# Block B's second feed-forward layer in seven quarter products instead of eight, with partial sums copied out by ScalarE and added by GpSimd

## The reference

```python
h2 = rmsnorm(x, p['norm_ffn_g'])
u = jnp.square(jax.nn.relu(jnp.einsum('btd,df->btf', h2, p['w_up'])))
x = x + jnp.einsum('btf,fd->btd', u, p['w_down'])
```

## Time and profile before

| | |
|---|---|
| median of 3 runs | 1424.47 us (1423.86 to 1426.74) |
| profiled execution, first to last instruction | 1424.1 us, clock 0.993 |
| TensorE busy | 1375.1 us (97%) |
| VectorE, ScalarE, GpSimd busy | 834.5, 542.6, 318.1 us |
| block B's 8 groups | about 1042 to 1415 us of the span |
| one group in the middle | 46.0 us |

### The profile page before, as it was taken

One profiled execution on the slowest core, in us unless ns is written; L12 is line 12 of the kernel. 1 busy time (PEld: TensorE's weight loads), 2 busy tenths in 40 slices (PEclk: granted clock), 3 DMA queues, 4 the chain that ended last, 5 costly groups with the idle time before them and its releaser, 6 DMA issues.

```text
span 1424.1 us, 23612 instructions
## 1 busy us (share of the span) xinstructions
PE 1375.1 (97%) x8781; PEld 1145.8 (80%) x8781; DVE 834.5 (59%) x1416; ACT 542.6 (38%) x1011; POOL 318.1 (22%) x363
## 2 busy tenths in 40 slices
PE   7998999999999999998999999999999999999998
PEld 6767777776777767776767767667999999999998
DVE  5469667745648886758667564444454455445542
ACT  6444332414546554533325241332442234223431
POOL 2546624435523534342000000000220000000000
PEclk9999999999999999999999999999999999999999
DMA  8547745434255553453377565971532233123311
GB/s 273 147 129 236 219 131 169 140 120 140 89 159 168 184 174 112 132 165 121 104 240 240 190 218 174 315 245 62 179 125 76 90 119 104 60 75 119 119 31 60
DMA packets 115635, 211.99 MB, mean 149 GB/s; under 512 B 12665, under 2 KB 45722, under 8 KB 115522
## 3 DMA queue, kind: packets, MB, share of 16 engines
q1 hardware_dynamic: 104306, 176.94, 38.3%
q10 hardware_dynamic: 11216, 33.57, 7.4%
HBM read 184.00 MB, written 26.46 MB: 148 GB/s over the span
## 4 chain that ended last, share of the span: by engine, by line
PE 64%; DVE 5%; ACT 3%; issue 2%; DMA 0%; ACTq 0%; POOL 0%; SPq 0%; DVEq 0%; POOLq 0%
PE ps L85 18%; PE ps L87 17%; PE ps L86 17%; PE ps L2634 2%; PE ps L1495 2%; PE ps L1532 2%; PE ps L1314 1%; DVE uw_l L2084 1%; PE ps L1516 1%; ACT uw_h L2080 1%; DVE ul L2243 1%; PE ps L1728 1%; DVE sd L2388 1%; DVE dl L2190 1%; DVE xr L2236 0%
## 5 line engine op out<-in xcount | busy, mean ns | idle before, releaser
L85 PE MATMUL ps<-uh,dh 128*128 128x512 f32 (+2 forms) x768 | 250.0, 326 | 5.0 <-DVE dl L2190 3.9
L87 PE MATMUL ps<-uh,dl 128*128 128x512 f32 (+2 forms) x768 | 245.4, 320 | 0.0
L86 PE MATMUL ps<-ul,dh 128*128 128x512 f32 (+2 forms) x768 | 245.0, 319 | 0.0
L2399 POOL TENSOR_TENSOR kr<-kr,qb 128x512 f32<-128x512 f32 x128 | 175.9, 1385 | 167.4 <-DMA kr<-in_cache_k 167.0
L2254 DVE TENSOR_TENSOR xt<-xt,ps 128x256 f32<-128x256 f32 (+2 forms) x192 | 97.6, 512 | 164.6 <-PE ps L87 164.1
L85 PEld LDWEIGHTS ps<-uh,dh 128*128 128x128 f32 x768 | 144.4, 188 | 25.3 <-DVE xt L2254 7.6
L87 PEld LDWEIGHTS ps<-uh,dl 128*128 128x128 f32 x768 | 144.5, 188 | 11.5
L86 PEld LDWEIGHTS ps<-ul,dh 128*128 128x128 f32 x768 | 144.6, 188 | 9.7
L2095 ACT ACTIVATE dh<-raw_dn 128x1024 fp32r<-128x1024 f32 x64 | 67.5, 1055 | 215.6 <-PE ps L87 214.9
L2080 ACT ACTIVATE uw_h<-raw_up 128x1024 fp32r<-128x1024 f32 x80 | 84.5, 1056 | 163.4 <-PE ps L87 163.3
L85 PE MATMUL ps<-x2hB,uw_h 128*128 128x264 f32 (+1 forms) x512 | 145.2, 284 | 0.7 <-DVE x2lB L2218 0.7
(11 more groups left out here) (339 smaller groups left out, 2840.0 us busy)
## 6 DMA issues: line engine op xcount, KB each, us to landing
kr<-in_cache_k SPq DMA_DIRECT2D x128, 256.0 KB, 3.1
raw_up<-in_w_up_units SPq DMA_DIRECT2D x64, 512.0 KB, 4.7
vr<-in_cache_v SPq DMA_DIRECT2D x128, 256.0 KB, 3.5
raw_dn<-in_w_down ACTq DMA_DIRECT2D x62, 512.0 KB, 3.6
raw<-in_w_in_units SPq DMA_DIRECT2D x23, 512.0 KB, 5.1
raw_up<-in_w_out_units SPq DMA_DIRECT2D x16, 512.0 KB, 4.4
xin<-in_x_prompt SPq DMA_DIRECT2D x8, 512.0 KB, 5.4
xt_scratch<-xts SPq DMA_DIRECT2D x8, 512.0 KB, 5.9
```

The lines of the kernel that those rows point to most:

```text
L85: pe.matmul(out, lh, rh, start=first and n == 0, stop=False)
L86: pe.matmul(out, lh, rl, start=False, stop=False)
L87: ins = pe.matmul(out, ll, rh, start=False, stop=last and n == len(ks) - 1)
L2399: pool.tensor_tensor(k[:, :], k[:, :], qb[v // PAGES][:, :], ALU.mult).then_inc(k_multiplied, 1)
```

## The change

`feed_forward` becomes two functions: `feed_first` for block A, with the same work in the same order, and `feed_last` for block B. The `out` tiles and `up` tiles of B are the same matmuls. `down` is replaced: the 512 x 1024 piece of `w_down` of a group is taken as a 2 x 2 matrix of quarters A11, A12, A21, A22 (256 hidden features x 512 outputs, A12 and A22 belonging to the second half of the hidden features, A21 and A22 to the second half of the outputs), the squared activations as 2 x 2 quarters U11 to U22 (256 features x 256 or 264 tokens), and their product is made from seven quarter products (Winograd's form) instead of eight. Each quarter product is 4 output tiles x 2 k-steps x 3 matmuls = 24 matmuls, so `down` has 168 instead of 192. P2 and P4 have 256 columns, the other five 264.

What this needs per group, by engine:

- GpSimd: four sums or differences of weight quarters (S1 = A21+A22, S3 = A11-A21, S2 = S1-A11, S4 = A12-S2; 128x1024 elements each), and 16 additions of partial results onto `xt` (128x256 or 128x264).
- ScalarE: 7 high parts of factors instead of 4 (128x1024), 8 squares as before, 14 high parts of activations instead of 8, and 16 new copies of a PSUM bank into SBUF (`read` into `held`).
- VectorE: 7 low parts of factors instead of 4, 8 relus as before, 8 differences of activations (T1 to T4, `change`, in place), 14 low parts instead of 8, and 12 additions from PSUM onto `xt` instead of 16.
- TensorE: P1 is left in its bank, P6, P7 and P4 are accumulated onto it, P3 onto P5. In between ScalarE reads the bank, and the next product of that bank waits for that read (`y_copied`). P6 of an output tile waits for the read of P1, P7 for that of P6, P4 for that of P7, P3 for that of P5.
- SyncE: the `w_down` tiles come on its queue, all four buffers at once; ScalarE no longer issues them.
- At the end one token tile is turned inside the last group and four behind it, each with its own PSUM banks and its own SBUF place; ScalarE copies three, VectorE two.

In groups 0 to 6 TensorE's order is P1 for all four output tiles, then P5, P6, P2, P7, P3, P4 for tiles 0 and 1, then the same for tiles 2 and 3. Cut to its core:

```diff
+PRODUCTS = {"P1": ("A11", "U11", "X"), "P2": ("A12", "U21", "Y"), "P3": ("S4", "U22", "Z"), "P4": ("A22", "T4", "X"),
+            "P5": ("S1", "T1", "Z"), "P6": ("S2", "T2", "X"), "P7": ("S3", "T3", "X")}
+BEGINS = ("P1", "P5", "P2")
+AFTER = {"P6": "P1", "P7": "P6", "P4": "P7", "P3": "P5"}
+READ_OUT = ("P1", "P6", "P7", "P5")
+ADDED = ("P2", "P3", "P4")
+def products(g):
+    if g == FGROUPS - 1:
+        return [(x, j) for x in ("P1", "P6", "P2", "P7", "P5", "P4", "P3") for j in range(PAIRS)]
+    return ([("P1", j) for j in range(PAIRS)]
+            + [(x, j) for js in ((0, 1), (2, 3)) for x in ("P5", "P6", "P2", "P7", "P3", "P4") for j in js])
...
+        def product(g, x, j):
+            name, part, kind = PRODUCTS[x]
+            if x in BEGINS:
+                take(pe, "down", (g, x, j))
+            else:
+                pe.wait_ge(y_copied, read_no(g, AFTER[x], j))
+            if j == 0:
+                pe.wait_ge(dn_low, factor_no(g, name))
+            f, n = slice(j * P, (j + 1) * P), width(x)
+            for k in range(2):
+                if j == 0:
+                    pe.wait_ge(u_low, low_no(g, part, k))
+                ins = split_matmuls(pe, ps[:, down_bank(g, kind, j), 0:n],
+                                    lambda k: (factor(fh, name)[:, k, f], factor(fl, name)[:, k, f]),
+                                    lambda k: (part_place(part, k, False)[:, 0:n], part_place(part, k, True)[:, 0:n]),
+                                    [k], x in BEGINS and k == 0, k == 1, x not in BEGINS)
+            ins.then_inc(down_ready, 1)
...
+        def read(g, x, j):
+            act.wait_ge(down_ready, product_no(g, x, j))
+            if held_before(g, x, j):
+                act.wait_ge(sq_added, held_before(g, x, j))
+            if (g, x, j) == (0, "P1", 0):
+                for i in range(2):
+                    act.wait_ge(sem(f"y_out{i}"), 32)
+            if (g, x, j) == (FGROUPS - 1, "P1", 2):
+                act.wait_ge(dn_low, factor_no(g, "S2"))
+                act.wait_ge(sq_added, sum_no(g, "S4"))
+            dst = held_at(g, x, j)
+            act.activation(dst, ps[:, down_bank(g, PRODUCTS[x][2], j), 0:256 if x == "P1" else WIDE], ACT.Copy).then_inc(y_copied, 1)
...
+            todo = reads(g)
+            high_factor(g, "A11")
+            high_factor(g, "A12")
+            if g == 0:
+                split_high(act, t + 2)
+                act.wait_ge(norm_product, 4)
+                for p in range(2):
+                    ins = act.activation(rb2[:, tokens(p)], ps[:, 7 - p, 0:HALVES[p][1]], ACT.Copy)
+                ins.then_inc(rb2_made, 1)
+            square(g, 0, 0)
+            high_part(g, "U11", 0)
+            square(g, 0, 1)
+            if g:
+                split_high(act, t + 2)
+            high_part(g, "T1", 0)
+            high_factor(g, "S1")
+            high_factor(g, "S3")
+            square(g, 1, 0)
+            high_part(g, "U11", 1)
+            square(g, 1, 1)
+            split_high(act, t + 3)
+            high_part(g, "T1", 1)
+            high_factor(g, "S2")
+            high_factor(g, "A22")
+            square(g, 2, 0)
+            high_part(g, "U21", 0)
+            square(g, 2, 1)
+            if more:
+                split_high(act, t + 4)
+            for name in ("U22", "T2", "T3", "T4"):
+                high_part(g, name, 0)
+            high_factor(g, "S4")
+            square(g, 3, 0)
+            high_part(g, "U21", 1)
+            square(g, 3, 1)
+            high_part(g, "T2", 1)
+            read(g, *todo[0])
+            read(g, *todo[1])
+            high_part(g, "T3", 1)
+            high_part(g, "U22", 1)
+            read(g, *todo[2])
+            read(g, *todo[3])
+            high_part(g, "T4", 1)
+            read(g, *todo[4])
+            read(g, *todo[5])
+            if more:
+                split_high(act, t + 5)
+            for what in todo[6:]:
+                read(g, *what)
...
+        def summed(g):
+            a11, a12, a21, a22 = (quarter(x) for x in ("A11", "A12", "A21", "A22"))
+            for x in range(FT):
+                pool.wait_ge(dn_in[x], raw_no(g, x))
+            if g == 0:
+                pool.wait_ge(sem("mix_turned"), 18)
+                pool.wait_ge(sem("ods_done"), 1)
+            else:
+                pool.wait_ge(dn_low, factor_no(g - 1, "S1"))
+            pool.tensor_tensor(s1[:, :, :], a21, a22, ALU.add).then_inc(sq_added, 1)
+            pool.tensor_tensor(a21, a11, a21, ALU.subtract).then_inc(sq_added, 1)
+            pool.wait_ge(dn_low, factor_no(g, "A11"))
+            pool.wait_ge(sq_added, sum_no(g, "S3"))
+            pool.tensor_tensor(a11, s1[:, :, :], a11, ALU.subtract).then_inc(sq_added, 1)
+            pool.wait_ge(dn_low, factor_no(g, "A12"))
+            pool.wait_ge(sq_added, sum_no(g, "S2"))
+            pool.tensor_tensor(a12, a12, a11, ALU.subtract).then_inc(sq_added, 1)
+        def add(g, x, j):
+            pool.wait_ge(y_copied, read_no(g, x, j))
+            if g and x in ("P1", "P6"):
+                pool.wait_ge(added, added_no(g - 1, "P2" if x == "P1" else "P3", j))
+            if x in ("P5", "P7") and both_before(g, x, j):
+                pool.wait_ge(sq_added, both_before(g, x, j))
+            o, c = out_tile(x, j)
+            pool.tensor_tensor(xt[:, o, c], xt[:, o, c], held_at(g, x, j), ALU.add).then_inc(sq_added, 1)
...
+            low_factor(g, "A11")
+            low_factor(g, "A12")
+            relu(g, 0, 0)
+            relu(g, 0, 1)
+            low_part(g, "U11", 0)
+            change(g, "T1", 0)
+            if g:
+                split_low(dve, t + 2)
+            low_part(g, "T1", 0)
+            low_factor(g, "S1")
+            low_factor(g, "S3")
+            relu(g, 1, 0)
+            relu(g, 1, 1)
+            low_part(g, "U11", 1)
+            change(g, "T1", 1)
+            split_low(dve, t + 3)
+            low_part(g, "T1", 1)
+            low_factor(g, "S2")
+            relu(g, 2, 0)
+            relu(g, 2, 1)
+            low_part(g, "U21", 0)
+            change(g, "T2", 0)
+            change(g, "T3", 0)
+            if more:
+                split_low(dve, t + 4)
+            low_part(g, "U22", 0)
+            change(g, "T4", 0)
+            low_part(g, "T2", 0)
+            low_part(g, "T3", 0)
+            low_part(g, "T4", 0)
+            low_factor(g, "A22")
+            relu(g, 3, 0)
+            relu(g, 3, 1)
+            low_part(g, "U21", 1)
+            change(g, "T2", 1)
+            change(g, "T3", 1)
+            low_part(g, "T2", 1)
+            change(g, "T4", 1)
+            low_part(g, "T3", 1)
+            low_part(g, "U22", 1)
+            low_part(g, "T4", 1)
+            low_factor(g, "S4")
+            todo = adds(g)
+            add(g, *todo[0])
+            add(g, *todo[1])
+            if more:
+                split_low(dve, t + 5)
+            for what in todo[2:]:
+                add(g, *what)
+        for t in (1, 3):
+            copy_y(t)
```

More of the change, by code:

```diff
@@ new lines, in up @@
+            take(pe, "up", g, x)
+            for i in range(2):
+                for k in range(i * KT // 2, (i + 1) * KT // 2):
+                    if g == 0 and x == 0:
+                        pe.wait_ge(x2_low, k + 1)
+                    ins = split_matmuls(pe, ps[:, bank("up", g, x), :], weights(t),
+                                        lambda k: (x2h[:, k, ALL], x2l[:, k, ALL]), [k], k == 0, k == KT - 1)
+                    if g == 0 and x == 1 and k == 4:
+                        spread()
+                if i:
+                    ins.then_inc(up_ready, 1)
+                beside(tick + i)
@@ new lines, in down @@
+            for o in range(2):
+                take(pe, "down", g, o)
+                sum_over(o, range(3), True, False)
+            for o in range(2):
+                pe.wait_ge(u_low, up_no(g, 3) + 1)
+                sum_over(o, range(3, 4), False, True).then_inc(down_ready, 1)
+            for i in range(2):
+                beside(tick + i)
+            for o in range(2, KT):
+                take(pe, "down", g, o)
+                sum_over(o, range(FT), True, True).then_inc(down_ready, 1)
+                beside(tick + o)
@@ L2054, in tensor @@
+        first_outs()
+        for u in range(2, KT):
             out(u)
@@ L2063, in tensor @@
             tick += KT
-        if part:
-            for t in range(2, 5):
-                turn_y(t)
     def before_tile(u, beside):
@@ L2223, in vector @@
                 t = KT + FT * g + x
-                more = t + 2 < TILES or part == 0
                 beside(tick + 2 * x)
@@ L2256, in feed_forward @@
     return {"sync": sync, "tensor": tensor, "scalar": scalar, "gpsimd": gpsimd, "vector": vector,
             "split_high": split_high, "split_low": split_low, "preload": preload}
+PAIRS = KT // 2
+HALVES = [(0, 256), (256, 264)]
+WIDE = 264
+FACTORS = ["A11", "A12", "S1", "S3", "S2", "A22", "S4"]
```

(3 more changed lines are left out.)

771 lines of the change are left out of this document (529 added, 242 removed).

## The result

The kernel after takes 1435.68 us (median of 4 runs, 1432.7 to 1437.7), the kernel before on the same chip 1425.56 (1423.86 to 1426.74): a ratio of 1.0065, 95% interval 1.0044 to 1.0085. The forecast was 1435. The profiled execution of after has a span of 1435.9 us.

A forecast was written before the change was run, and what follows sets the result against it. TensorE was taken to bound block B, its saving eaten by stalls: 1424.1 + 10 (group 0) + 3 (groups 1 to 6) - 0.4 (last group) - 2.4 (end) = 1434.3, plus 0.4 from span to median: 1435 us. Range 1405 to 1458, 8 in 10.

The forecast's parts named there:

- The matmuls: TensorE's down in block B: fewer matmuls save 2.8 us a group, 22 us for the eight.
- rival 3: Accumulating onto a bank read in between costs TensorE its pitch, 168 matmuls last as long as 192: 1457 us, chance 0.05.
- The middle group: Groups 1 to 6 of block B: stalls of 3.3 us against 2.8 saved, 46.5 us a group, +3 in all.
- All four stalls: TensorE's waits in a middle group: up tile 2 0.5 us, tile 3 0.7, P6 0.8, P7 1.3.
- Turns: GpSimd and VectorE alternate at the shared SBUF port; a 1024-element sum on GpSimd holds it 2.35 us.
- rival 1: GpSimd doesn't get between VectorE's queued operations, so the port harms little: 1408 us, chance 0.34.
- The price of a sum: GpSimd's durations: 2.5 us for a sum of 1024 elements, about 0.75 for an addition of 264.
- rival 2: VectorE becomes the bound through dearer sums, pieces and hand-overs: 2.3 us more a group, 1455 us, chance 0.18.
- Group 0: Block B's first group, whose up results wait for the norm: stalls sum to 13.3 us, net +10.
- The spread: TensorE's step behind group 0's norm: waits 4.2 us because GpSimd's S1 and S3 delay VectorE's diagonal operations.
- The last group and the end: Last group -0.4 us; behind the last product fewer turns of token tiles remain, -2.4 us.
- The 0.4 us between span and median: Added to the forecast span of 1434.3 us to reach the forecast median of 1435.

The follow-up runs named there:

- The kernel without collisions: Changed kernel with GpSimd's four weight sums made over 16 columns instead of 1024, all waits kept, results wrong: 1409.71 us, ratio 0.9894.
- narrow sums: Changed kernel with GpSimd's four weight sums over 16 columns instead of 1024, all waits kept, results wrong: 1409.71 us, ratio 0.9894.
- filled sums: Changed kernel with each GpSimd weight sum replaced by three constant fills of about its length that read no SBUF, results wrong: 1410.47 us, ratio 0.989.
- narrow sums and narrow adds: Changed kernel with GpSimd's four sums over 16 columns of 1024 and its 16 additions over 8 columns, results wrong: 1406.22 us, ratio 0.9868.

## Why the prediction was right

**The matmuls (rival 3).** 2.8 us a group forecast, 2.7 measured. Accumulating onto a bank that was read in between costs nothing that these runs show, so rival (3) falls.

**The middle group.** 46.5 forecast, 46.36 measured. All four stalls were where the working had put them, behind the operations it had named. With the 0.27 us that a wait costs beyond its bracket, tile 3 lost 0.7 us (0.7 forecast), P6 0.7 (0.8) and P7 1.4 (1.3). Tile 2 lost 0.3 (0.5): 0.18 before its first matmul, which starts 0.30 behind the last one where the pitch is 0.12, and 0.1 behind it. Together 3.1 us, where 46.36 - 43.32 is 3.0 and 3.3 was forecast.

**Turns (rival 1).** The two low parts at 1150.24 decide it: GpSimd does get between two queued operations of VectorE. The kernel without collisions took 1409.71, where rival (1) had put 1408.

**The price of a sum (rival 2).** 2.5 us assumed, 2.41 measured undisturbed (1157.48 to 1159.89, the fourth sum of the group above). Additions of 264: 0.75 assumed, 0.75 to 0.76 measured. A middle group of 46.36, under the 46.5 without surcharges, leaves no room for rival (2)'s 2.3 us.

**Group 0.** The total was nearly right and its parts weren't. From the anchor to tile 3 of group 1 are 73.6 us, before 63.8: +9.8, where +10 and group 1's 0.5 and 0.7 were forecast, 11.2. The spread waits 3.74 (forecast 4.2), tile 3 waits 3.94 instead of 6.8, P6 0.28 and P7 nothing, instead of 1.0 and 1.3. What the sum lacked is the clock: 0.58 behind the spread's wait and 0.56 behind tile 3's. The first 29 matmuls should last 1.04 + 25 x 0.12 = 4.0 us and lasted 6.36, 2.3 us longer; the next 19 lasted 3.8 instead of 2.3, 1.5 longer. The 2.3 cost nothing of themselves: tile 3's low part was done when VectorE had it done, 27.3 us behind the anchor (forecast 28.2), and TensorE merely came later and waited less. The kernel with A22's low part later bears this out: there the spread ran at the upper level (1.14 us instead of 2.10), tile 3 waited 4.83 instead of 3.94, and it started 27.3 us behind the anchor all the same. The 1.5 are real and stand where the forecast had P6 and P7. So two errors, stalls oversized and a clock that the prediction put at nothing, mostly cancel; that is luck.

**The last group and the end.** From tile 3 of group 7 to the end: 36.3 us after, 39.5 before, -3.2. The forecast's -0.4 and -2.4 hold 1.2 us of up stalls that lie ahead of this stretch, so its figure here is -4.0. P6 lost 0.8 us instead of 1.2, and the store took 3.7 us (1435.9 - 1432.2) instead of the 2.4 taken from before. (The forecast's own parts behind the last product, 3.7, 1.0 and 2.4, add up to 7.1 and not to its 7.4.)

**The sum.** From the anchor +8.7 us in the trace (9.8, 2.1 and -3.2), and 10.2 forecast for the same stretch (11.2, 3 and -4.0). The spans differ by 11.8; the other 3.1 lie ahead of the anchor (1044.77 before, 1047.85 after), in block A, which is the same in both. The other kernels with the same block A reach the anchor between 1043.4 and 1046.2, so this is how executions differ, and not the change. The medians differ by 10.1. The 0.4 us between span and median was no constant: here the median lies 0.2 under the profiled span, since every run of after takes 1.7 us more than its own span and the profiled one took 1437.59. So the mechanism was right, while 1435 against 1435.68 is closer than its terms were.

**Left open.** Whether tile 3 of group 0 could be reached without a wait: it takes a place for low T1, S1 and S3 that VectorE doesn't have between the relus, and no run tried to give some of them to ScalarE or GpSimd.

## What to carry to other kernels

An engine with nothing to do isn't free if it shares a port with the one that the work is taken to spare: write the port's turns into the lists of both engines, and put long operations where the other has slack. When a chain is full, the removal of one wait brings out the next one behind it (2 us later when P7's went, at tile 3 when the spread's went); what gained here was moving the same work to a real gap and ordering it as it is used. A saving on the engine that bounds is worth its full price only if all others stay ahead of it at every hand-over, and working the lists out by hand for one period found those places here before a run did.

## What was not expected of the hardware

TensorE's clock fell to its lower level behind every single wait of 3.74 us or more in block B of these profiles (up to 9.29) and stayed there for 3 to 6 us of full work. Behind 3.3 us it went either way at the same place, tile 3 of group 0. With narrow sums, behind a wait of 3.28 us, and with filled sums, behind 3.30 us:

```profile
1064.10:1068.10 4.00, 4.00 (x34) 4.00 (x35) 3.25 (x8) 3.08 (x6) 0.00 (x0) 1.00 0.42 137
...
1066.70:1070.70 4.00, 4.00 (x19) 4.00 (x20) 3.26 (x8) 3.07 (x6) 0.00 (x0) 0.50 0.42 137
```

With narrow sums and narrow adds, the same list up to there and a wait of 3.29 us, it fell as well (0.57 in the 4 us behind it). So the wait's length alone doesn't decide it, and a single profile doesn't settle what a wait costs. Matmuls without use kept the clock up through a gap in which it otherwise fell, in the one profile taken.

GpSimd's fills leave VectorE's subtractions alone (2.35 us for two) but not its multiplications of one tensor (2.33 us for five that take 1.02). The one blocked by the port isn't always the one that the profile shows idle: the time lies inside the operation's duration (4.83 for two low parts, 3.42 for a sum of 2.41), so it is read from durations, not from waits.
